# Seven of nine RMS norms: sum of squares split in two rounded halves, summed by ones on TensorE, root on ScalarE, reciprocal on VectorE

## The reference

```python
def rmsnorm(x, g):
    xf = x.astype(jnp.float32)
    y = xf * lax.rsqrt(jnp.mean(xf * xf, axis=-1, keepdims=True) + EPS)
    return (y * g.astype(jnp.float32)).astype(x.dtype)

def swiglu(h, w_gate, w_up, w_down):
    return (jax.nn.silu(h @ w_gate) * (h @ w_up)) @ w_down
...
    for i in range(DEPTH):
        x = x + 0.5 * swiglu(rmsnorm(x, norm_ff1[i]), ff1_w_gate[i], ff1_w_up[i], ff1_w_down[i])
        x = x + token_mixer(rmsnorm(x, norm_mix[i]), w_in[i], ...)
        x = x + 0.5 * swiglu(rmsnorm(x, norm_ff2[i]), ff2_w_gate[i], ff2_w_up[i], ff2_w_down[i])
        g = jax.nn.sigmoid(rmsnorm(x, norm_ple[i]) @ ple_w_gate[i])
        x = x + g * (p[i] @ ple_w_proj[i])
    return rmsnorm(x, norm_final)
```

## Time and profile before

| | before |
|---|---|
| median of 3 runs | 1181.16 us (1180.98 to 1181.28) |
| profiled execution, span from first to last instruction | 1179.5 us |
| TensorE busy | 1168.9 us, 99% of the span |
| VectorE busy | 814.0 us, 69% |
| ScalarE busy | 593.7 us, 50% |
| GpSimd busy | 122.8 us, 10% |
| mean granted TensorE clock | 0.997 of full |

### The profile page before, as it was taken

The page is one execution under the profiler, slowest core; times in us unless marked ns, Lnnn a source line. Parts: engine busy times, 40 slices in busy tenths (PEclk is TensorE's granted clock), DMA queues, the critical chain, the costliest instruction groups (busy, mean ns, idle before and its releaser), DMA issues.

```text
span 1179.5 us, 24037 instructions
## 1 busy us (share of the span) xinstructions
PE 1168.9 (99%) x10534; PEld 1144.7 (97%) x10534; DVE 814.0 (69%) x939; ACT 593.7 (50%) x669; POOL 122.8 (10%) x136
## 2 busy tenths in 40 slices
PE   9999999999999999999999999999999999999997
PEld 9999999999999999999999999999899999999996
DVE  5866555688978766655786665558798777666455
ACT  5544445555745544444554444447367455444443
POOL 2000001011512000001210000100133020000011
PEclk9999999999999999999999999999999999999998
DMA  7655555545445555555555555554635365555541
GB/s 288 235 203 188 193 201 177 184 156 202 145 149 207 190 188 206 183 204 187 179 202 194 194 199 184 197 203 139 214 140 169 118 235 203 184 204 186 186 172 36
DMA packets 33384, 218.87 MB, mean 186 GB/s; under 512 B 5184, under 2 KB 6016, under 8 KB 7296
## 3 DMA queue, kind: packets, MB, share of 16 engines
q1 hardware_dynamic: 33280, 217.34, 53.2%
HBM read 216.15 MB, written 1.05 MB: 184 GB/s over the span
## 4 chain that ended last, share of the span: by engine, by line
PE 98%; DVE 1%; DMA 1%; ACT 0%; issue 0%; POOL 0%; SPq 0%; POOLq 0%; DVEq 0%
PE psum L385 31%; PE psum L387 31%; PE psum L386 31%; PE psum L665 1%; PE psum L644 1%; DMA x_all<-in_x 1%; PE psum L517 0%; PE psum L578 0%; PE psum L628 0%; PE psum L699 0%; PE psum L424 0%; PE psum L710 0%; PE psum L613 0%; DVE gates L1671 0%; PE psum L733 0%
## 5 line engine op out<-in xcount | busy, mean ns | idle before, releaser
L1222 DVE TENSOR_TENSOR w_lo<-raw,w_hi 128x2048 fp32r<-128x2048 f32 x200 | 457.9, 2293 | 213.5 <-ACT w_hi L856 213.4
L856 ACT ACTIVATE w_hi<-raw 128x2048 fp32r<-128x2048 f32 x201 | 385.2, 1917 | 366.6 <-PE psum L387 360.8
L385 PE MATMUL psum<-hA_hi,w_hi 128*128 128x256 f32 x1360 | 377.9, 278 | 0.0
L386 PE MATMUL psum<-hA_hi,w_lo 128*128 128x256 f32 x1360 | 375.7, 276 | 0.0
L387 PE MATMUL psum<-hA_lo,w_hi 128*128 128x256 f32 x1360 | 375.7, 276 | 0.0
L385 PEld LDWEIGHTS psum<-hA_hi,w_hi 128*128 128x128 f32 x1360 | 255.4, 188 | 2.7 <-issue 2.7
L386 PEld LDWEIGHTS psum<-hA_hi,w_lo 128*128 128x128 f32 x1360 | 255.4, 188 | 0.0
L387 PEld LDWEIGHTS psum<-hA_lo,w_hi 128*128 128x128 f32 x1360 | 255.3, 188 | 0.0
L385 PE MATMUL psum<-hB_hi,w_hi 128*128 128x256 f32 x832 | 230.3, 277 | 1.1 <-DVE w_lo L1654 1.1
L386 PE MATMUL psum<-hB_hi,w_lo 128*128 128x256 f32 x832 | 229.7, 276 | 0.0
L387 PE MATMUL psum<-hB_lo,w_hi 128*128 128x256 f32 x832 | 229.7, 276 | 0.0
(11 more groups left out here) (182 smaller groups left out, 1226.0 us busy)
## 6 DMA issues: line engine op xcount, KB each, us to landing
raw<-in_weights SPq DMA_DIRECT2D x203, 1024.0 KB, 4.9
raw<-in_weights SPq DMA_DIRECT2D x2, 512.0 KB, 6.2
out<-gates SPq DMA_DIRECT2D x3, 256.0 KB, 2.2
x_all<-in_x SPq DMA_DIRECT2D x1, 520.0 KB, 3.9
x_all<-in_x SPq DMA_DIRECT2D x1, 512.0 KB, 6.2
relu<-in_p SPq DMA_DIRECT2D x2, 256.0 KB, 5.0
consts<-in_consts SPq DMA_DIRECT2D x1, 384.0 KB, 5.7
out<-gates SPq DMA_DIRECT2D x2, 128.0 KB, 2.3
```

Source lines behind the costliest of these rows:

```text
L385: pe.matmul(o, lh, rh, start=start, stop=False)
L386: pe.matmul(o, ll, rh, start=False, stop=False)
L856: act.activation(w_hi[:, s, :], raw[:, s, :], ACT.Copy).then_inc(hi_ready[s], 1)
L1222: dve.tensor_tensor(w_lo[:, s, :], raw[:, s, :], w_hi[:, s, :].bitcast(F32), ALU.subtract).then_inc(lo_ready[s], 1)
```

## The change

For seven norms (all but the mixers') the way from total to rb is another one. The squares are now scaled by 1/32 before squaring, so total holds parts of the mean, in all nine norms. ScalarE rounds total to fp32r into diag_hi (round_total), VectorE puts total minus that into diag_lo (rest_total), and TensorE multiplies 128 x 128 ones by both, 256 columns each (mean_everywhere): the mean in every partition in one go. ScalarE takes it from PSUM with EPS as bias and Sqrt, back into total (root); VectorE writes the reciprocal into rb (inverse_root). The one-column sums, the power on GpSimd and the diagonal are gone there. Before the next norm GpSimd waits for rb_ready before it writes total.

In the FFNs mean_everywhere stands in the middle of the third chunk, in layer 0 too; in the embedding it stands in the middle of the first gate chunk. In the last norm total and the two last squares are multiplied as three fp32 matmuls of 256 columns that add up in PSUM; VectorE, and no longer ScalarE, squares the last tile; the last two tiles are not scaled by ScalarE beforehand but take gain and rb in one VectorE instruction each.

```diff
+ROOT = 1 / 32
...
+            def mean_everywhere(L, k, b):
+
+                pe.wait_ge(total_lo, of_root(L, k))
+                added_everywhere(b)
+
             def spread(L, k, b):
 
-                pe.wait_ge(diag_done, L * 4 + k + 1)
-                if L == L_N:
-                    pe.matmul(bank[b][:, 0:T], ones[:, :], diag[:, :, :].rearrange("p a t -> p (a t)"), start=True, stop=True
-                              ).then_inc(rb_sum, 1)
-                    return
+                pe.wait_ge(diag_done, L + 1)
+                added_everywhere(b)
+
+            def added_everywhere(b):
+
                 pe.matmul(bank[b][:, 0:T], ones_r[:, :], diag_hi[:, :, :].rearrange("p a t -> p (a t)"), start=True, stop=False)
                 pe.matmul(bank[b][:, 0:T], ones_r[:, :], diag_lo[:, :, :].rearrange("p a t -> p (a t)"), start=False, stop=True
...
-                    if m == 3 and not first:
-                        token_sums(L, k, 4)
...
                     if q == 2:
-                        token_sums(L, k, 4) if first else spread(L, k, 4)
-                    if q == 3 and first:
-                        spread(L, k, 4)
+                        mean_everywhere(L, k, 4)
                     by_columns(s, b, h, (1,)).then_inc(chunk_done[s], 1)
...
-                token_sums(L, 3, 7)
...
                     if i < 3:
-                        by_columns(s, bank[4 + i], hA).then_inc(chunk_done[s], 1)
+                        by_columns(s, bank[4 + i], hA, (0,))
+                        if i == 0:
+                            mean_everywhere(L, 3, 7)
+                        by_columns(s, bank[4 + i], hA, (1,)).then_inc(chunk_done[s], 1)
...
-                for t in range(2):
-                    half = slice(t * P, (t + 1) * P)
-                    mm = pe.matmul(bank[4][:, T + t:T + t + 1], last_squared[:, c - 1, half] if c else total[:, half], ones[:, 0:1],
-                                   start=c == 0 and t == 0, stop=c == 2, skip_group_check=True)
-            mm.then_inc(sums_done, 1)
-            spread(L_N, 0, 4)
+                mm = pe.matmul(bank[4][:, 0:T], ones[:, :], last_squared[:, c - 1, :] if c else total[:, :], start=c == 0, stop=c == 2)
+            mm.then_inc(rb_sum, 1)
...
+            def round_total(L, k):
+
+                act.wait_ge(sq_added, of_norm(L, k, 4) + START)
+                act.activation(diag_hi[:, :, :].rearrange("p a t -> p (a t)"), total[:, :], ACT.Copy).then_inc(total_hi, 1)
+
+            def root(L, k, b):
 
                 act.wait_ge(rb_sum, L * 4 + k + 1)
+                act.activation(total[:, :], bank[b][:, 0:T], ACT.Sqrt, bias=eps[:, 0:1]).then_inc(rooted, 1)
...
                     if g == 0:
+                        round_total(L, 2 * f)
                         split(L, n + 4)
-                        take_rb(L, 2 * f, 4)
+                        root(L, 2 * f, 4)
...
+                round_total(L, 3)
                 split(L, PROJ + 3)
-                take_rb(L, 3, 7)
+                root(L, 3, 7)
...
+                    if last and c:
+                        continue
                     act.wait_ge(x_done if c else tile_added, (L * 16 + 16) if c else (L + 1))
                     if last:
-                        act.activation(last_squared[:, c, :], x[:, 6 + c, :], ACT.Square).then_inc(last_squares, 1)
+                        act.activation(last_squared[:, c, :], x[:, 6 + c, :], ACT.Square, scale=ROOT).then_inc(last_squares, 1)
                     else:
                         act.activation(hB[0][:, 6 + c, :], x[:, 6 + c, :], ACT.Copy, scale=gains[:, 4, 6 + c:7 + c]
                                        ).then_inc(h_hi_ready if c else tile_hi, 1)
                 if last:
-                    for c in range(2):
-                        act.activation(final[:, 6 + c, :], x[:, 6 + c, :], ACT.Copy, scale=gains[:, 4, 6 + c:7 + c]).then_inc(final_scaled, 1)
+                    root(L_N, 0, 4)
...
-                pool.wait_ge(mean_done, L * 4 + k + 1)
-                pool.tensor_tensor(rstd[:, :], mean[:, :], half_neg[:, 0:2], ALU.pow).then_inc(rstd_done, 1)
+                if k == 1:
+                    pool.wait_ge(mean_done, L + 1)
+                    pool.tensor_tensor(rstd[:, :], mean[:, :], half_neg[:, 0:2], ALU.pow).then_inc(rstd_done, 1)
+                elif pairs == 4:
+                    pool.wait_ge(rb_ready, L * 4 + k + 1)
...
+            def rest_total(L, k):
+
+                dve.wait_ge(total_hi, of_root(L, k))
+                dve.tensor_tensor(diag_lo[:, :, :].rearrange("p a t -> p (a t)"), total[:, :],
+                                  diag_hi[:, :, :].bitcast(F32).rearrange("p a t -> p (a t)"), ALU.subtract).then_inc(total_lo, 1)
+
+            def inverse_root(L, k):
+
+                dve.wait_ge(rooted, of_root(L, k))
+                dve.reciprocal(rb[:, :], total[:, :]).then_inc(rb_ready, 1)
+                dve.wait_ge(rb_ready, L * 4 + k + 1)
...
-                        if L == 0 and f == 0:
-                            dve.wait_ge(const_landed, 16)
-                        mean_square(L, 2 * f, 4)
+                        rest_total(L, 2 * f)
+                        inverse_root(L, 2 * f)
                         split(L, n + 4)
-                        dve.wait_ge(rb_ready, L * 4 + 2 * f + 1)
...
+                rest_total(L, 3)
                 split(L, PROJ + 3)
-                dve.wait_ge(rb_ready, L * 4 + 4)
+                inverse_root(L, 3)
...
-                    mean_square(L, 4, 4)
+                    dve.wait_ge(x_done, L * 16 + 16)
+                    dve.scalar_tensor_tensor(out=last_squared[:, 1, :], in0=x[:, 7, :], scalar=ROOT * ROOT, in1=x[:, 7, :],
+                                             op0=ALU.mult, op1=ALU.mult).then_inc(last_squares, 1)
...
+            inverse_root(L_N, 0)
             for m in STORES:
                 n = m.stop - m.start
-                dve.tensor_tensor(final[:, m, :], final[:, m, :], bank[4][:, 0:T].unsqueeze(1).to_broadcast([P, n, T]), ALU.mult
+                if n == 1:
+                    dve.scalar_tensor_tensor(out=final[:, m.start, :], in0=x[:, m.start, :], scalar=gains[:, 4, m], in1=rb[:, :],
+                                             op0=ALU.mult, op1=ALU.mult).then_inc(out_ready, 1)
+                    continue
+                dve.tensor_tensor(final[:, m, :], final[:, m, :], rb[:, :].unsqueeze(1).to_broadcast([P, n, T]), ALU.mult
```

More of the change, by code:

```diff
@@ L123, in hybrid_trunk @@
         diag_lo = sb("diag_lo", [P, 2, P], F32R)
-        diag = total.rearrange("p (a t) -> p a t", a=2)
         ones_r = sb("ones_r", [P, P], F32R)
@@ L149, in hybrid_trunk @@
         gbias = sb("gbias", [P, 2])
+        eps = sb("eps", [P, 1])
         wi = sb("wi", [P, 2, 8])
@@ L234, in hybrid_trunk @@
         rb_sum = sem("rb_sum")
+        total_hi = sem("total_hi")
+        total_lo = sem("total_lo")
+        rooted = sem("rooted")
         rb_ready = sem("rb_ready")
@@ L252, in hybrid_trunk @@
         last_squares = sem("last_squares")
-        final_scaled = sem("final_scaled")
         out_ready = sem("out_ready")
@@ L315, in of_norm, with of_root @@
             return (L * 4 + k) * 4 + pair
+        def of_root(L, k):
+            return L * 3 + max(k, 1)
         def piece(i):
@@ L440, in ffn @@
                 k = 2 * f
-                first = L == 0 and f == 0
                 s = operands(L, off) if f else turn(L, off)[0]
@@ L816, in embed @@
                         pairs(s, LAST_TILES[1] - 1, hA, 1, range(8)).then_inc(chunk_done[s], 1)
-                    if i == 0:
-                        spread(L, 3, 7)
             start_counts(pe, chunk_done)
@@ L865, in squares @@
                 act.wait_ge(sq_added, of_norm(L, k, m) + START)
-                act.activation(squared[:, :, :], x[:, 2 * m:2 * m + 2, :], ACT.Square).then_inc(sq_done, 1)
+                act.activation(squared[:, :, :], x[:, 2 * m:2 * m + 2, :], ACT.Square, scale=ROOT).then_inc(sq_done, 1)
             def take_pair(L, k, m, h, squares_too=True):
@@ L887, in split_pieces, with take_rb @@
                     act.activation(w_hi[:, s, piece(i)], raw[:, s, piece(i)], ACT.Copy).then_inc(piece_hi if i < 3 else hi_ready[s], 1)
-            def take_rb(L, k, b):
+            def round_total(L, k):
+                act.wait_ge(sq_added, of_norm(L, k, 4) + START)
+                act.activation(diag_hi[:, :, :].rearrange("p a t -> p (a t)"), total[:, :], ACT.Copy).then_inc(total_hi, 1)
+            def root(L, k, b):
                 act.wait_ge(rb_sum, L * 4 + k + 1)
+                act.activation(total[:, :], bank[b][:, 0:T], ACT.Sqrt, bias=eps[:, 0:1]).then_inc(rooted, 1)
+            def take_rb(L, b):
+                act.wait_ge(rb_sum, L * 4 + 2)
                 act.activation(rb[:, :], bank[b][:, 0:T], ACT.Copy).then_inc(rb_ready, 1)
@@ L925, in mix @@
                 split(L, MIX + 3)
-                take_rb(L, 1, 6)
+                take_rb(L, 6)
```

(25 more changed lines are left out.)

2 lines of the change are left out of this document (removed).

## The result

The changed kernel takes 1206.61 us (median of 4 runs, 1206.56 to 1206.64) where the kernel before, beside it, takes 1181.22 (1180.98 to 1181.35): a ratio of 1.0215, 95% interval 1.0201 to 1.0228. It is 25.4 us slower; forecast were 1179.5 us and no difference that can be measured.

What follows compares the result with a forecast made beforehand. TensorE, without waits from 12 to 1168 us, was taken to bound the kernel, then a serial chain at the end. 1181.16 - 2.9 (sums) + 2.9 (new wait) - 1.7 (end) = 1179.5 us, range 1178.7 to 1182.0.

Steps and rivals of the forecast that it cites:

- What bounds the kernel: TensorE never waits from 12 to 1168 us; only matmuls added or removed and new waits count there.
- The sums: Two one-column fp32 matmuls go from each of six norms: 5 x 0.47 + 0.56 = 2.9 us off TensorE.
- The wait in the first norm: Layer 0: TensorE stands from 22.24 to 25.05 for VectorE's subtraction behind a weight split; +2.9 us.
- The five others covered: The same wait in the other five norms is ready before TensorE comes; smallest margins 1.3 and 1.5 us.
- The root and the reciprocal inside the stream: ScalarE's extra table loads and VectorE's later splits in the FFNs are hidden by slack; 0 us.
- The end: Serial chain behind the last product: first output multiply at 1172.3 instead of 1174.05; -1.7 us, reciprocal taken as 0.42.
- Rival 1: Reciprocal takes eight steps an element, 2.29 us, so the end becomes +0.15 and the time 1181.3 us; chance 0.30.
- Rival 2: TensorE's clock falls during the new wait in the first norm, near 4 us at half: +1.9, 1181.4 us; chance 0.10.
- The sum: Whole kernel: 1181.16 - 2.9 + 2.9 - 1.7 = 1179.5 us; chance 0.50.

Runs made afterwards that it cites:

- e8: e5 with the six norms' pairs of one-column sums put back at their old places as unused work; 1184.95 us.
- e6: e1 with VectorE subtracting ahead of the split instead of behind it, in the first FFN of layer 0 only; 1179.1 us.
- e1: The changed kernel with eps in the unused rest of half_neg's line, so no tensor behind it moves; 1182.1 us.
- e5: e1 with the first FFN's spreading products in layer 0 moved from the third chunk back to the fourth; 1182.22 us.
- e7: e5 with the last norm's reciprocal over 64 of its 256 columns, other tokens' outputs not the reference's; 1180.73 us.
- e3: The changed kernel with its eps, padding ahead of hB 16 words shorter, so hB and hid are back in their places; 1182.13 us.
- e2: The kernel before with one unused 64-byte tensor where the changed kernel has eps, nothing else; 1207.23 us.
- e9: e5 with VectorE's split of chunk n+4 ahead of the reciprocal in the first FFN of layer 0; 1179.21 us.
- e13: The kernel before with the very first padding 64 bytes longer, so all tensors move together; 1181.6 us.
- e4: The kernel before with hB and hid 512 bytes further; 1181.18 us.

## Why the prediction was wrong

**What bounds the kernel** was read rightly: TensorE without slack from 12 us to the last product. The inference from it failed: "two things alone count there: matmuls added or removed, and any wait that the change creates". There is a third, how long each of the remaining ones takes, and it cost 26 us, about nine times the largest term of the sum. The prediction went through the diff's instructions and never through its tensors; the line with eps has no cost in it, not even one of zero. The listing did show paddings named after places, and at 99% busy a few ns on each of ten thousand products count in full; but no row of the kernel before could have told what a shift costs.

**The sums, -2.9**: held (e8: 2.7; e6: its last product comes 2.1 earlier than in the earlier trace rows with a wait of 0.8, so 2.9).

**The wait in the first norm, +2.9**: right in place and cause, and 2.7 in e1. The 0.1 that it added for the pipeline to fill is there too: behind the wait the second product starts 0.22 us after the first, not 0.11. In the changed kernel the wait is 2.1, since TensorE, slowed by then, comes to it later.

**The five others covered**: held; the changed kernel has no other wait in the stream.

**The root and the reciprocal inside the stream, 0**: held at the forecast's placement, but with less margin than was counted, since the reciprocal takes 1.75 and not 0.42. In the FFNs the Silu, with its table loaded, waits a further 3.45 us for VectorE, where before it followed its load by 0.02 to 0.3; TensorE did not feel it. In e5, one chunk later, it did.

**The end, -1.7**: mis-sized, -0.25. The fp32 product took 0.70 (0.65 taken), the root 0.47 (0.46), the reciprocal 1.75 (0.42). The choice between 0.42 and 2.29 was made from a 2-column row: 160 ns for a reciprocal, 163 for a multiply. By the two widths of e7, two columns cost 0.154 + 0.012 = 0.17, so that row could not tell them apart. Rival 1 was nearer: six steps of 1.05 ns to a column, where the Trainium skill ("VectorE: DVE Perf Modes", First, the fixed hardware budget) speaks of a repeat count of 8.

**Rival 2, the clock**: real in seven of eleven executions of e1 and in nine of ten of e3, at 1.5 us between e1's groups (1.9 forecast). In the changed kernel, where the wait is 2.1 us, the clock stayed at 1.00. The length of the fall, 4 us, was read from TensorE's first products, but the earlier trace rows show the clock at 1.00 there, so that row said nothing about it; that e1 has 3.4 us is luck. The argument against the rival, that the clock had stayed full for 3.6 us at the end, did not hold in the middle of the stream.

**The sum.** The last product: -2.9 + 2.1 + 26.4 = +25.6, the 26.4 being what is left for the placement; e2 alone gave 26.0. The 0.4 between them is not explained; e2's own executions spread over 0.6 us. With hB and hid in their places and the clock up, the terms as measured give 1181.3 - 2.9 + 2.7 - 0.25 = 1180.8, and e1's faster group stands at 1180.7: the change would then have been within 0.2% of before, in the forecast's range, but above the forecast itself, because the reciprocal eats the gain at the end.

## What to carry to other kernels

Read a diff for the tensors that it allocates as well as for its instructions: where a tensor is added ahead of an operand of a matmul stream, work out whether the operand moves against the weights, and put small tensors in unused parts of lines that are there. If TensorE's busy time rises while its count falls and its clock stays, compare the mean duration by moving operand before looking for waits. And do not price a wide instruction from a row with two columns: the fixed part hides the slope.

When a slow step is put in front of a queue, moving its consumer later does not help if other work stands between them; reordering that queue did (e6, e9).

## What the runs showed of the hardware

- An fp32r product of 256 columns starts every 0.112 us when its moving operand lies 192 bytes past w_hi modulo 512, and every 0.118 at a distance of 256; at 0 TensorE's busy time rises as much as at 256 (26.6 and 26.5 us for 4608 products), at 128 by 23.1, at 320 by 16.5. Equal shifts of both do nothing (e13), nor does one of 512 (e4).
- VectorE's reciprocal costs 6.2 ns a column and 0.154 us: 1.75 us for 256 columns, 0.553 for 64.
- After TensorE had stood for 2.6 to 2.7 us between dense products (e1, e3, e5), the granted clock fell to its lower level of 1.2 GHz, in e1 for 3.4 us, in most executions (seven of eleven, nine of ten and seven of eleven, by the groups of their times); in the traced execution of e7 the same wait of 2.6 us left it at 1.00. After 2.1 and 0.8 us (the changed kernel, e6) it did not fall. What decides between the outcomes is not shown.
